# Meta keys of a head pair: products with the identity into two partition groups, and one matmul with a block-diagonal value tile

## What is computed

```python
META, HEAD_DIM = 16, 64
h = jnp.concatenate([meta_tokens, x], axis=1)
for l in range(DEPTH_2):                       # 2 layers
    h = h + 0.5 * swiglu(rms_norm_2(h, ffn1_norm[l]), ffn1_w_in[l], ffn1_w_out[l])
    h = h + hybrid_mixer(rms_norm_2(h, mix_norm[l]), ...)
    h = h + 0.5 * swiglu(rms_norm_2(h, ffn2_norm[l]), ffn2_w_in[l], ffn2_w_out[l])

# inside each branch: probabilities over 16 meta keys and the token keys, times the values
p = jax.nn.softmax(jnp.concatenate([s_meta, s_win], axis=-1), axis=-1)
o = (jnp.einsum('bnhgqm,bmhd->bnqhgd', p[..., :META], vm)
     + jnp.einsum('bnhgqk,bnkhd->bnqhgd', p[..., META:], vb))
```

## Time and profile before

| | us |
|---|---|
| median of 3 runs | 1780.38 (1780.17 to 1781.73) |
| the profiled execution | 1781.34 |
| its span, first to last instruction | 1779.5 |

### The profile page before, as it was taken

How to read it: one execution, slowest core, us unless ns; L and a number is a source line. 1 busy time by engine, 2 the same in 40 slices (tenths; PEclk the granted TensorE clock), 3 DMA queues, 4 the chain that set the end, 5 groups by cost and what they waited for, 6 DMA issues and landing times.

```text
span 1779.5 us, 36917 instructions
## 1 busy us (share of the span) xinstructions
PE 1728.5 (97%) x13968; PEld 1667.6 (94%) x13968; DVE 1181.1 (66%) x2060; ACT 813.7 (46%) x1299; POOL 265.2 (15%) x261
## 2 busy tenths in 40 slices
PE   7999999999999999999999999999999899999996
PEld 6989999999999998788999999999999788999996
DVE  7567756767665576665886656766566566787755
ACT  4555444544444433445544443544433454555442
POOL 1020000011000203332320001000111333330012
PEclk9999999999999999999999999999999999999998
DMA  7425555555555543342455554555554243455553
GB/s 263 134 94 177 185 179 188 187 179 182 173 177 173 171 166 119 115 133 97 155 178 176 174 169 167 189 168 174 178 169 151 84 143 119 155 185 184 186 188 108
DMA packets 83943, 288.79 MB, mean 162 GB/s; under 512 B 9088, under 2 KB 16000, under 8 KB 83456
## 3 DMA queue, kind: packets, MB, share of 16 engines
q1 hardware_dynamic: 79488, 283.14, 47.9%
q10 hardware_dynamic: 4352, 4.20, 0.8%
HBM read 285.96 MB, written 1.34 MB: 161 GB/s over the span
## 4 chain that ended last, share of the span: by engine, by line
PE 87%; DVE 7%; ACT 3%; issue 1%; POOL 1%; DMA 0%; ACTq 0%; POOLq 0%; SPq 0%; DVEq 0%
PE PS L837 26%; PE PS L839 26%; PE PS L838 26%; DVE w_lo L1468 2%; PE PS L1304 1%; PE PS L1340 1%; ACT S_all L713 1%; ACT w_hi L444 1%; PE PS L1344 1%; PE PS L1312 1%; DVE x_lo L1473 0%; DMA h<-xT 0%; PE PS L1031 0%; PE PS L1329 0%; PE PS L1322 0%
## 5 line engine op out<-in xcount | busy, mean ns | idle before, releaser
L1468 DVE TENSOR_TENSOR w_lo<-raw,w_hi 128x1024 fp32r<-128x1024 f32 x525 | 655.8, 1250 | 315.7 <-ACT w_hi L444 305.6
L837 PE MATMUL PS<-x_hi,w_hi 128*128 128x272 f32 (+1 forms) x2832 | 825.4, 291 | 11.8 <-DVE x_lo L1473 10.8
L839 PE MATMUL PS<-x_hi,w_lo 128*128 128x272 f32 (+1 forms) x2832 | 814.9, 288 | 0.0
L838 PE MATMUL PS<-x_lo,w_hi 128*128 128x272 f32 (+1 forms) x2832 | 812.7, 287 | 0.0
L444 ACT ACTIVATE w_hi<-raw 128x1024 fp32r<-128x1024 f32 x525 | 551.5, 1056 | 546.5 <-PE PS L839 540.7
L837 PEld LDWEIGHTS PS<-x_hi,w_hi 128*128 128x128 f32 x2832 | 539.9, 191 | 18.6 <-issue 15.8
L838 PEld LDWEIGHTS PS<-x_lo,w_hi 128*128 128x128 f32 x2832 | 539.8, 191 | 0.7
L839 PEld LDWEIGHTS PS<-x_hi,w_lo 128*128 128x128 f32 x2832 | 540.3, 191 | 0.0
L837 PE MATMUL PS<-a_hi,w_hi 128*128 128x272 f32 (+1 forms) x1280 | 366.1, 286 | 4.9 <-DVE a_lo L368 3.7
L839 PE MATMUL PS<-a_hi,w_lo 128*128 128x272 f32 (+1 forms) x1280 | 365.1, 285 | 0.0
L838 PE MATMUL PS<-a_lo,w_hi 128*128 128x272 f32 (+1 forms) x1280 | 364.3, 285 | 0.0
(11 more groups left out here) (285 smaller groups left out, 1237.8 us busy)
## 6 DMA issues: line engine op xcount, KB each, us to landing
raw<-stream SPq DMA_DIRECT2D x525, 512.0 KB, 3.3
biasB<-rpbz ACTq DMA_DIRECT2D x16, 256.0 KB, 3.2
G<-b1mats SPq DMA_DIRECT2D x2, 1024.0 KB, 7.3
h<-xT SPq DMA_DIRECT2D x1, 1088.0 KB, 7.8
out<-qk SPq DMA_DIRECT2D x8, 128.0 KB, 2.1
mat<-mats SPq DMA_DIRECT2D x1, 952.0 KB, 5.3
v_tok<-u_rows SPq DMA_DIRECT2D x4, 142.0 KB, 3.1
mat<-u_rows SPq DMA_DIRECT2D x4, 142.0 KB, 3.8
```

The source lines that it names most:

```text
L837: pe.matmul(ps, hi, rh, start=first, stop=False)
L838: pe.matmul(ps, hi, rl, start=False, stop=False)
L839: return pe.matmul(ps, lo, rh, start=False, stop=last)
L1468: dve.tensor_tensor(w_lo[:, slot, :], raw[:, slot, :], w_hi[:, slot, :].bitcast(F32), ALU.subtract).then_inc(lo_done, 1)
```

## The change

It touches the meta keys alone.

- **turn1.** The four transposes of the meta columns become four matmuls with the identity. Their output goes to partitions 64 to 79 (head 0) and 96 to 111 (head 1) of bank 7, 256 columns in place of 512, in the order query tile, then head.
- **turned1** (VectorE). The second copy is 64x256 (partitions 64 to 127) in place of 16x512.
- **pv.** The two meta products become one, with 64 contraction rows (partitions 64 to 127), 128 stationary columns and 256 moving ones. The value tile is block-diagonal: rows 64 to 79 hold head 0's meta values in its 64 columns, rows 96 to 111 head 1's in the other 64, all else is zero.
- **Values.** Behind the three transposes of each value tile two matmuls with the identity bring the meta piece to partitions 64 to 79 and 96 to 111 as well; VectorE copies the half that belongs to each head there, two copies of 16x64, with step waits between the copies. The copy to partitions 0 to 15 stays (the meta queries use it).
- **Once:** a memset of the lower half of `v_tok[:, 2, :]` ahead of the layers.

```diff
--- before.py
+++ after.py
@@ -199,7 +199,8 @@
         S4 = S_all[:, 0:8 * ST].rearrange("p (u b q t) -> p u b q t", u=2, b=2, q=2)
         Sm = G[:, 21, :]
         PT_b = [PT[:, 0:512], PT[:, 512:1024]]
-        PT2 = PT[:, 1024:1536]
+        PT2 = PT[:, 1024:1280]
+        MB = 64
         PTm, PTm2 = Gf[:, 22 * L:22 * L + 256], Gf[:, 22 * L + 256:22 * L + 384]
         q_meta = Gf[:, 22 * L + 384:22 * L + 512].rearrange("p (a b) -> p a b", a=2)
         minp, sump, snkp, denp = (att[:, 8 * i:8 * i + 8] for i in range(4))
@@ -1271,7 +1272,11 @@
                             vs = vstage[i % 2]
                             pe.transpose(PS[:, b, 0:P], vs[:, 0:P], ident)
                             pe.transpose(PS[:, b, P:2 * P], vs[:, P:2 * P], ident)
-                            mm = pe.transpose(PS[0:META, b, 2 * P:3 * P], vs[:, 2 * P:L], ident)
+                            pe.transpose(PS[0:META, b, 2 * P:3 * P], vs[:, 2 * P:L], ident)
+                            for u in range(2):
+                                r = MB + 32 * u
+                                mm = pe.matmul(PS[r:r + META, b, 3 * P:4 * P], vs[:, 2 * P:L], ident, start=True, stop=True,
+                                               skip_group_check=True)
                         elif what == "sumC":
                             pe.wait_ge(c_squared, l * 5 + 5)
                             for e in range(5):
@@ -1324,10 +1329,11 @@
                     if p > 0:
 
                         pe.wait_ge(o_lo_done, l * PAIRS + p)
-                    for b in range(2):
-                        for qt in range(2):
-                            mm = pe.transpose(PS[0:META, 7, b * SEQ + qt * P:b * SEQ + (qt + 1) * P],
-                                              S4[:, p % 2, b, qt, SEQ:L], ident)
+                    for qt in range(2):
+                        for b in range(2):
+                            r = MB + 32 * b
+                            mm = pe.matmul(PS[r:r + META, 7, qt * P:(qt + 1) * P], S4[:, p % 2, b, qt, SEQ:L], ident,
+                                           start=True, stop=True, skip_group_check=True)
                     mm.then_inc(turned1_out, 1)
 
                 def pv(p):
@@ -1338,12 +1344,10 @@
                         for b in range(2):
                             vc = v_column(typ, t, b)
                             pe.matmul(PS[64 * b:64 * b + 64, 7, 0:SEQ], v_tok[:, kt, vc:vc + 64],
-                                      PT_b[b][:, kt * SEQ:(kt + 1) * SEQ], start=(kt == 0), stop=False)
-                    for b in range(2):
-                        vc = v_column(typ, t, b)
-                        mm = pe.matmul(PS[64 * b:64 * b + 64, 7, 0:SEQ], v_tok[0:META, 2, vc:vc + 64],
-                                       PT2[0:META, b * SEQ:(b + 1) * SEQ], start=False, stop=True)
-                    mm.then_inc(pv_out, 1)
+                                      PT_b[b][:, kt * SEQ:(kt + 1) * SEQ], start=(kt == 0), stop=False, skip_group_check=True)
+                    vc = v_column(typ, t, 0)
+                    pe.matmul(PS[:, 7, 0:SEQ], v_tok[MB:P, 2, vc:vc + P], PT2[MB:P, :], start=False, stop=True,
+                              skip_group_check=True).then_inc(pv_out, 1)
 
                 def m_scores(m):
 
@@ -1913,6 +1917,8 @@
                 ob += 2 * MOE_HALF + KD
             assert ax.n == B1_AUX
 
+            dve.memset(v_tok[MB:P, 2, :], 0.0).then_inc(setup_done, 1)
+            dve.wait_ge(setup_done, 2)
             dve.memset(biasB[:, :, :, SEQ:L], 0.0).then_inc(setup_done, 1)
             dve.wait_ge(tables_landed, 16)
 
@@ -1954,8 +1960,15 @@
                         elif what == "v":
                             step(dve.tensor_copy(v_tok[:, 0:2, i * P:(i + 1) * P],
                                                  PS[:, b, 0:2 * P].rearrange("p (k c) -> p k c", k=2)))
-                            dve.tensor_copy(v_tok[0:META, 2, i * P:(i + 1) * P], PS[0:META, b, 2 * P:3 * P])\
-                               .then_inc(aux_free, ax.up())
+                            step(dve.tensor_copy(v_tok[0:META, 2, i * P:(i + 1) * P], PS[0:META, b, 2 * P:3 * P]))
+                            for u in range(2):
+                                r, at = MB + 32 * u, 64 * u
+                                ins = dve.tensor_copy(v_tok[r:r + META, 2, i * P + at:i * P + at + 64],
+                                                      PS[r:r + META, b, 3 * P + at:3 * P + at + 64])
+                                if u == 0:
+                                    step(ins)
+                                else:
+                                    ins.then_inc(aux_free, ax.up())
                         elif what == "sumC":
                             dve.tensor_scalar(G[0:10, 8, :], PS[0:10, b, 0:L], 1.0 / HD, EPS, ALU.mult, ALU.add)\
                                .then_inc(aux_free, ax.up())
@@ -2044,7 +2057,7 @@
 
                     dve.wait_ge(turned1_out, l * PAIRS + p + 1)
                     dve.tensor_copy(PT_b[1], PS[:, 6, 0:512]).then_inc(probsT_dve, 1)
-                    dve.tensor_copy(PT2[0:META, :], PS[0:META, 7, 0:2 * SEQ]).then_inc(probsT_dve, 1)
+                    dve.tensor_copy(PT2[MB:P, :], PS[MB:P, 7, 0:SEQ]).then_inc(probsT_dve, 1)
 
                 def gate_out(j):
```

## The result

| | before | after | ratio, 95% interval |
|---|---|---|---|
| medians beside each other | 1781.06 (4 runs) | 1788.96 (4 runs) | 1.0053 (1.0035 to 1.0070) |
| again, on another chip | 1779.58 (15 runs) | 1788.58 (6 runs) | 1.0054 (1.0037 to 1.0071) |
| profiled execution, its span | 1781.34, 1779.5 | 1788.56, 1786.7 | |

The change costs 7.9 us, 0.53%. The forecast was 1788.0, +7.6, slower. In the changed kernel the gate products are L838 to L840, the value tile's transposes L1273 to L1275 and its new products L1278, `turn1`'s L1327 and L1335, `pv`'s L1346 and the single meta product L1349, the scores L1309 and L1317 head 0's transposes; VectorE's two copies are L2059 and L2060.

The account below looks back on a forecast made before the run. TensorE, busy 97% of the span and 87% of the chain, bounds the kernel. Pairs' turn1 and stalls +2.5, pv -1.1, values +6.2 make +7.6 us: median 1780.38 becomes 1788.0, range 1782 to 1794.

Parts of the forecast that it names:

- The values, +6.2 us: Value tiles, 12 times: two added identity products cost TensorE 0.52 us each, with no wait to hide it.
- `turn1` uncovered, +0.28 a pair: turn1, 24 pairs: identity products in place of transposes take 0.85 us, not 0.57, hidden only by stalls in pv.
- `pv`, -0.15, +0.05 and +0.15: Single meta product: -0.15 us in 12 pairs with scores next, +0.05 in 11, +0.15 in one; together -1.1.
- The stalls' cover: Ten pairs where pv waits for VectorE's copy: waits and a copy ending 0.25 earlier hide turn1's cost, -1.4 us.
- The pairs together: All 24 pairs: turn1 less the stalls' cover, +2.5 us, and pv, -1.1 us.
- The sum: Whole kernel: 2.5 - 1.1 + 6.2 = +7.6 us, median 1788.0; chance 0.67.
- Nothing covered: Rival: pv's stall travels with the later turn1, or the narrower copy is no faster; +11.8 us, 1792.2, chance 0.09.
- Twice the slots: Rival: 16-column products do not run side by side, or take four slots each; +20.2 us, 1800.6, chance 0.11.
- Half the price: Rival: tiles this small pay half the price of a change of form; +0.4 us, 1780.8, chance 0.08.
- no price: Rival: no change of form is paid around the new products; -6.8 us, 1773.6, chance 0.05.

Follow-up runs that it names:

- the copy over all partitions: The changed kernel with VectorE's last copy over all 128 partitions (128x256) in place of the upper 64; measured 1787.99 in one run.
- the doubled products: The changed kernel with each of turn1's identity products issued twice to the same output; measured 1798.03, ratio 1.0099 to the kernel before.
- the bursts: The changed kernel with turn1's products split, query tile 0 ahead of head 1's transposes, tile 1 behind; measured 1792.60, ratio 1.0073 to the kernel before.
- both parts by themselves: Two runs: the kernel before with only the value part, 1787.74, ratio 1.0048; the changed kernel without the value part, 1783.45, ratio 1.0024.
- the padded rows: The kernel before with pv's two meta products reading all 128 rows, rows 16 to 127 set to zero; measured 1775.24, ratio 0.9973.

## Why the prediction was right

- **The values, +6.2 us.** Measured 6.27 in the traces, the same in each. The step was exact, with its 0.52 a tile and no cover.
- **`turn1` uncovered, +0.28 a pair.** 0.30 to 0.31, counted as the forecast does. The mechanism was right, the size a little small: 0.65 us too little over 24 pairs.
- **`pv`, -0.15, +0.05 and +0.15.** From the last gate product ahead of `pv` to the first behind the scores, in pairs without a stall: 0.15 saved where scores follow at once, 0.02 to 0.05 lost elsewhere, 0.19 lost in the one pair of the old form. One pair did far better, -0.73, of which 0.44 was its stall: there the small transposes of the meta queries start beside the meta product, which I had counted as an ordinary change of form. Changed kernel:

```profile
760.37 0.48 PE L1349 MATMUL PS<-PT,v_tok 64*128 64x256 f32 x1
760.38 0.34 PE L1369 MATMUL PS<-mat,G 48*16 48x48 f32 x4
```

- **The stalls' cover.** Ten waits, 3.8 us, have become one of 0.2 us and a few too short to be listed. The mechanism was right. The size of the copy's gain was off: 0.25 was taken as the difference of two lengths, but what counts is the end of the second copy against the start of the first, 1.27 before and 1.15 after, so 0.12. It matters only where the wait is longer than what `turn1` and the copy take off it, in four of the ten pairs, and costs the forecast some 0.5 us there (the copy over all partitions wins that much back).
- **The pairs together.** 2.5 - 1.1 = 1.4 forecast, 2.2 in the traces. `turn1`'s size (+0.65) and the copy's (+0.5) make the difference, less 0.3 for the pair with the small transposes.
- **The sum.** 6.27 + 2.2 = 8.5 at full clock, 7.2 in the profiled execution, 7.9 and 9.0 in the medians; +7.6 forecast. The steps were right in kind and near in size, but that the first median came within 0.3 us is luck in part: one stretch at the lower clock is 1.5 us, and the prediction left the clock out.
- **The rivals.** *Nothing covered* fell with the waits. *Twice the slots* fell with the doubled products. *Half the price* and *no price* fell with the trace after (0.20 from L1275 to L1278 where a slot is 0.108) and with the bursts.

Open: why both parts by themselves add up to more than the whole in the medians. The traces show no such surplus in the stretches of the change.

## What to carry to other kernels

Count the form of a matmul (rows by columns of its tile) as a state of TensorE: here each change costs about 0.09 us and the first weight load, on the way in and again on the way out. It is the tile of the array that counts, not the operand's width: a transpose of 16 columns kept the full form. Small products should take the form of their neighbours, by zero rows or by columns that nobody reads; two products in different partition groups already run side by side, so merging them into a block-diagonal one saves no work (what it saved here, 0.15 us where scores follow, came from the form). And take a part's preparation as seriously as the part: six value tiles a layer cost more than twelve pairs.

## What the hardware did that was not expected

- Products of one form on the two row halves of the array start out of program order: the next scores' first record (1464.06) starts ahead of the meta product's second (1464.37), which the program issues first.
- VectorE's copy of 64 partitions that starts on partition 64 does not overlap the one ahead of it: 0.72 between starts, 0.60 for a copy over all partitions.
- GpSimd's scaling of the probabilities (L2208, now L2221) fell from 1647 to 1135 ns in the mean, and VectorE's weight split beside it grew. The two go together: in the trace before, 18 of the 48 scalings take 2.45 us where all others but two take 1.09, and the splits beside them take 1.20; in the trace after no scaling takes over 2.2 us, and 19 splits take some 1.9 (as at 1462.82). Such a split starts 0.27 us behind the scaling and ends 1.09 behind the scaling's end, as if it had waited. The trace with the copy over all partitions has 2.15 us in those places, and the padded rows, with the copy of 16x512, show the picture of before. So the copy ahead decides which of the two is held up; what they share is only argued here. TensorE waits for neither in these places.
